# Hybrid decoder block on one core: where the state enters the chunk solve of the gated delta rule, the order of the first loads and masks, and the gate columns' operands

## The reference

```python
proj = xn @ w_in                       # q, k, v, z, and 8 narrow gate columns a, b (4 heads each)
g = -exp(a_log) * softplus(a + dt_bias);  beta = sigmoid(b)
# per chunk, gc = cumsum(g):
T = inverse(I + strict_lower((k * beta) @ k.T * decay))
u = T @ (v * beta)
w = T @ (k * beta * exp(gc))
v_new = u - w @ state
o = (q * exp(gc)) @ state + attn_qk @ v_new
state = state * exp(g_last) + (k * exp(g_last - gc)).T @ v_new
```

## Time and profile before

| | |
|---|---|
| median of three runs | 3064.27 us (3062.66 to 3067.36) |
| the profiled execution: its own time | 3064.6 us |
| its span, first to last instruction | 3062.9 us |
| mean granted clock of PE in it | 0.995 |
| busy: PE, PE's weight loads, DVE, ACT, POOL | 2977.1, 2469.3, 1606.3, 1077.6, 1260.9 us |

### The profile page before, as it was taken

The page is one execution under the profiler, slowest core; times in us unless marked ns, Lnnn a source line. Parts: engine busy times, 40 slices in busy tenths (PEclk is TensorE's granted clock), DMA queues, the critical chain, the costliest instruction groups (busy, mean ns, idle before and its releaser), DMA issues. The chain is left out here.

```text
span 3062.9 us, 42230 instructions
## 1 busy us (share of the span) xinstructions
PE 2977.1 (97%) x14494; PEld 2469.3 (81%) x14494; DVE 1606.3 (52%) x2186; ACT 1077.6 (35%) x1990; POOL 1260.9 (41%) x1126
## 2 busy tenths in 40 slices
PE   6999999999999999999999999999999899999998
PEld 6887788888887888878888878888888788887887
DVE  1454555545357444445565556554635744444445
ACT  4522445424233333332232244443423433332212
POOL 7322444442215444554342244444321454445443
PEclk9999999999999999999999999999999999999999
DMA  6622322241112222252322322214111122225231
GB/s 221 220 89 93 104 69 68 65 163 55 55 69 69 84 84 84 83 192 97 132 92 93 103 93 81 71 62 159 62 43 74 63 82 82 82 82 192 83 110 76
DMA packets 131685, 297.40 MB, mean 97 GB/s; under 512 B 11824, under 2 KB 52848, under 8 KB 131568
## 3 DMA queue, kind: packets, MB, share of 16 engines
q1 hardware_dynamic: 69072, 226.07, 21.3%
q10 hardware_dynamic: 62496, 69.78, 6.6%
HBM read 222.37 MB, written 73.43 MB: 97 GB/s over the span
## 5 line engine op out<-in xcount | busy, mean ns | idle before, releaser
L2385 DVE TENSOR_TENSOR h<-h,PS 128x1024 f32<-128x1024 f32 x272 | 330.9, 1220 | 333.8 <-PE PS L2564 214.8
L2562 PE MATMUL PS<-act_hi,w_hi 128*128 128x512 f32 (+1 forms) x1088 | 428.9, 394 | 10.5 <-POOL w_lo L2027 4.6
L1523 DVE TENSOR_TENSOR copied<-copied,PS 128x512 f32<-128x512 f32 x308 | 207.5, 686 | 400.8 <-PE PS L2564 387.8
L2564 PE MATMUL PS<-act_hi,w_lo 128*128 128x512 f32 (+1 forms) x1088 | 406.7, 374 | 0.0
L2563 PE MATMUL PS<-act_lo,w_hi 128*128 128x512 f32 (+1 forms) x1088 | 405.7, 373 | 0.0
L2013 POOL TENSOR_TENSOR w_lo<-raw,w_hi 128x256 fp32r<-128x256 f32 (+1 forms) x144 | 198.3, 1400 | 433.9 <-ACT w_hi L2104 433.9
L603 POOL TENSOR_TENSOR part_lo<-sum_s,part_hi 128x512 fp32r<-128x512 f32 x176 | 229.9, 1308 | 229.2 <-ACT part_hi L1055 229.2
L2562 PE MATMUL PS<-down,mid 128*128 128x512 f32 x704 | 276.4, 393 | 7.3 <-DVE h L2385 7.3
L2562 PE MATMUL PS<-op_t_hi,part_hi 128*128 128x512 f32 x704 | 275.1, 391 | 0.0
L2564 PE MATMUL PS<-down,mid 128*128 128x512 f32 x704 | 274.8, 390 | 0.0
L2563 PE MATMUL PS<-down,mid 128*128 128x512 f32 x704 | 274.5, 390 | 0.0
(11 more groups left out here) (334 smaller groups left out, 6161.7 us busy)
## 6 DMA issues: line engine op xcount, KB each, us to landing
raw<-in_w_units SPq DMA_DIRECT2D x156, 512.0 KB, 4.0
gu_raw<-in_w_units SPq DMA_DIRECT2D x64, 512.0 KB, 5.0
a_d<-copied SPq DMA_DIRECT2D x88, 256.0 KB, 2.2
mid_raw<-a_d SPq DMA_DIRECT2D x44, 512.0 KB, 4.2
qkvz_d<-stage ACTq DMA_DIRECT2D x64, 256.0 KB, 2.5
raw<-att_d SPq DMA_DIRECT2D x32, 512.0 KB, 3.2
h<-in_x SPq DMA_DIRECT2D x12, 1024.0 KB, 7.9
prep_raw<-in_w_units SPq DMA_DIRECT2D x16, 512.0 KB, 4.4
```

Of the source, the lines that this page charges most:

```text
L1523: dve.tensor_tensor(buf[dst][:, :], buf[a][:, :], bank(k), ALU.add)\
L2385: dve.tensor_tensor(h[:, t, :], h[:, t, :], flat(bank(b + 2 * (t % 2), 2)), ALU.add)\
L2562: nc.tensor.matmul(out_ap, whi, xhi, start=start, stop=False)
L2564: return nc.tensor.matmul(out_ap, wlo, xhi, start=False, stop=stop)
```

## The change

Three edits.

1. **State first.** The step w multiplies the keys `kqn` with `state` into bank 7, four matmuls, and needs nothing of `Xm`. DVE, in the step x6, multiplies the result with nbeg and adds it to `vb`, head by head (four operations). The step v is then `Xm x vb` alone, four matmuls instead of eight. The product `kbg` on DVE and the copy `wt` on ACT are gone.
2. **Start order.** SP loads `mem_in` and `gain` first and the small loads (and `w_ab`) after the first four weight units; ACT takes the statistics of the memory tiles as soon as these two have landed, and splits the first two weight units before the high halves of the memory tiles. POOL makes 14 constants, then goes to the Newton steps and weight halves; masks, `ones_r` and `wab_lo` come after the third Newton step of x. PE starts its transposes after 14 constants.
3. **Gate columns.** High and low part of each row block's eight columns lie side by side in one tile `wab`, so one stationary operand takes both; two matmuls (with `act_hi` and `act_lo`) per row block instead of three. DVE adds the two groups of eight result columns ("sum").

The core of the diff:

```diff
+        def wab_part(hl):
+            return wab[:, 0:KT * 16].rearrange("p (k s c) -> p k s c", s=2, c=8)[:, :, hl, :]
+        def wab_in():
+            return raw[2][:, 0:KT * 8].rearrange("p (k c) -> p k c", c=8)
...
                 if step == "w":
-                    act.wait_ge(S["w_full"], n + 1)
-                    act.wait_ge(S["vn_full"], n)
-                    act.activation(hflat(wt[:, :, :]), bank(7), ACT.Copy).then_inc(S["wt_ready"], 1)
                     if not last:
                         exp_decays(act, n + 1, 1 - par)
...
+            parts = bank(6, 2).rearrange("p b (t c) -> p (b t) c", t=4)
+            step("copy", lambda: dve.tensor_copy(gate_ab[:, :, :], parts[:, :, 2 * NH:4 * NH]))
+            step("sum", lambda: dve.tensor_tensor(gate_ab[:, :, :], gate_ab[:, :, :],
+                                                  parts[:, :, 0:2 * NH], ALU.add))
...
             dve.wait_ge(S["rn_ready"], n + 1)
-            dve.wait_ge(S["gram_full"], n)
+            dve.wait_ge(S["ks_full"], n)
...
+                if step == "x6":
+                    dve.wait_ge(S["ks_full"], n + 1)
+                    for hh in range(NH):
+                        last_rest = dve.scalar_tensor_tensor(
+                            vb[:, hh, :], r4(bank(7))[:, hh, :],
+                            G["nbeg"][:, bass.ds(m, 1), hh:hh + 1].rearrange("p n h -> p (n h)"),
+                            vb[:, hh, :], ALU.mult, ALU.add)
+                    last_rest.then_inc(S["vrest_ready"], 1)
                 if step == "x1":
-                    dve.wait_ge(S["kt_full"], n + 1)
-                    dve.wait_ge(S["w_full"], n)
-                    dve.tensor_tensor(kbg[:, :, :], r4(bank(7)), gate("nbeg", m), ALU.mult)\
-                        .then_inc(S["kbg_ready"], 1)
...
             if step == "w":
-                pe.wait_ge(S["x_ready"], (n + 1) * LEVELS)
-                pe.wait_ge(S["kbg_ready"], n + 1)
+                pe.wait_ge(S["s_ready"], n * 4)
...
                 for hh in range(NH):
-                    t = nc.tensor.matmul(r4(bank(7))[:, hh, :], kbg[:, hh, :], Xm[:, hh, :],
+                    t = nc.tensor.matmul(r4(bank(7))[:, hh, :], kqn[:, hh, 0, :], state[:, hh, :],
                                          start=True, stop=True)
...
             if step == "v":
                 pe.wait_ge(S["ym_ready"], (n + 1) * 12)
-                pe.wait_ge(S["wt_ready"], n + 1)
-                pe.wait_ge(S["s_ready"], n * 4)
+                pe.wait_ge(S["x_ready"], (n + 1) * LEVELS)
+                pe.wait_ge(S["vrest_ready"], n + 1)
                 for hh in range(NH):
-                    nc.tensor.matmul(r4(bank(3))[:, hh, :], Xm[:, hh, :], vb[:, hh, :],
-                                     start=True, stop=False)
-                    t = nc.tensor.matmul(r4(bank(3))[:, hh, :], wt[:, hh, :], state[:, hh, :],
-                                         start=False, stop=True)
+                    t = nc.tensor.matmul(r4(bank(3))[:, hh, :], Xm[:, hh, :], vb[:, hh, :],
+                                         start=True, stop=True)
...
+            sp.dma_start(mem_in[:, :, :], mem.rearrange("(t p) c -> p t c", p=P))\
+                .then_inc(S["gain_in"], 16)
             sp.dma_start(gain[:, :], g_mem[0:1, :].broadcast_to([P, D])).then_inc(S["gain_in"], 16)
...
             for n in range(4 * KT):
+                if n == 4:
+                    load_small()
...
+            pool.wait_ge(made(), FIRST_CONSTS)
+            newton(pool, 0, 0)
+            newton(pool, 1, 1)
+            for n in range(2 * KT):
+                split_lo_prep(n, n % RING)
+            for t in range(3):
+                newton(pool, norm_no(0, 0, t), t % 2)
+            build_masks()
+            pool.wait_ge(S["wab_hi_ready"], 3)
+            pool.tensor_tensor(wab_part(1), wab_in(), wab_part(0).bitcast(f32), ALU.subtract)\
+                .then_inc(S["wab_lo_ready"], 1)
...
+            for t in range(3, TT):
+                newton(pool, norm_no(0, 0, t), t % 2)
...
             act.preload_act_table_set("natural_log_exp_and_others")
-            act.wait_ge(S["const_in"], 8 * 16)
...
+            act.wait_ge(S["gain_in"], 2 * 16)
             for t in range(2):
                 norm_stats(mem_in[:, t, :], junk[:, :], t, t)
-            for t in range(2):
-                norm_hi(t, 0)
...
                 split_hi_prep(n, n % RING)
+                if n == 1:
+                    for t in range(2):
+                        norm_hi(t, 0)
...
+            act.wait_ge(S["const_in"], 7 * 16)
+            act.activation(nega[:, :], nega[:, :], ACT.Exp).then_inc(S["wab_hi_ready"], 1)
...
-            pe.wait_ge(S["const_made"], CONSTS + 1)
+            pe.wait_ge(S["const_made"], FIRST_CONSTS)
...
                     for k in range(KT):
-                        ks = slice(k * 8, k * 8 + P)
+                        ks = slice(k * 16, k * 16 + P)
                         cs = slice(c * CH, (c + 1) * CH)
-                        last = three(PS[:, 4 + c, :], wab_hi[:, ks], wab_lo[:, ks],
-                                     act_hi[:, k, cs], act_lo[:, k, cs], k == 0, k == KT - 1)
+                        nc.tensor.matmul(PS[:, 4 + c, :], wab[:, ks], act_hi[:, k, cs],
+                                         start=k == 0, stop=False)
+                        last = nc.tensor.matmul(PS[:, 4 + c, :], wab[:, ks], act_lo[:, k, cs],
+                                                start=False, stop=k == KT - 1)
```

More of the change, by code:

```diff
@@ L52 @@
 CONSTS = 36
+FIRST_CONSTS = 14
 GD = {n: i + 1 for i, n in enumerate(
-    "copy a neg min bmin w1 wm eq mx rc l1 l2 l3 sp g b1 b2 gc gl fd nb nn".split())}
+    "copy sum a neg min bmin w1 wm eq mx rc l1 l2 l3 sp g b1 b2 gc gl fd nb nn".split())}
 GATE_DVE = len(GD)
@@ L132, in block_kernel @@
         gain = sb("gain", [P, D])
-        wab_hi = sb("wab_hi", [P, KT * 8 + P], f32r)
-        wab_lo = sb("wab_lo", [P, KT * 8 + P], f32r)
+        wab = sb("wab", [P, KT * 16 + P], f32r)
         cw = sb("cw", [P, NH, 3, 4])
@@ L208, in block_kernel @@
         am = sb("am", [P, 2, NH, P // 2], at=z)
-        kbg = sb("kbg", [P, NH, P], at=z)
+        z[0] += NH * P * 4
         kdec = sb("kdec", [P, NH, P], at=z)
@@ L497, in gains @@
         def gains(half, which):
-            return 16 * (2 + NORM_ORDER.index((half, which)))
+            return 16 * (3 + NORM_ORDER.index((half, which)))
         def transposed(half, which):
@@ L1361, in chunk_dve @@
                 if step == "x2":
+                    dve.wait_ge(S["kt_full"], n + 1)
                     dve.wait_ge(S["kv_full"], n)
@@ L1984, in _ @@
                 n += 1
[L1987 to L1995, removed]
-                n += 1
[L1997 to L2000, removed]
-                triangle(v, 2 * b - 1, [[2 * b, m], [0, b]], -1)
-                n += 1
@@ L2003, in _, with build_masks @@
-            pool.memset(Ym[:, :, :], 0.0).then_inc(made(), 1)
-            n += 1
-            assert n == CONSTS
+            def build_masks():
+                n = FIRST_CONSTS
+                for l in range(LEVELS):
+                    b = 1 << l
+                    m = P // (2 * b)
+                    if l == 0:
+                        v = first_mask[:, :].rearrange("p (m e c) -> p m e c", e=2, c=b)[:, :, 0, :]
+                    else:
+                        v = even_mask[:, l - 1, :].rearrange("p (m c) -> p m c", c=b)
+                    pool.wait_ge(made(), n)
+                    pool.memset(v, 1.0).then_inc(made(), 1)
+                    n += 1
+                    pool.wait_ge(made(), n)
+                    triangle(v, -b, [[-2 * b, m], [0, b]], 1)
+                    n += 1
+                    pool.wait_ge(made(), n)
+                    triangle(v, 2 * b - 1, [[2 * b, m], [0, b]], -1)
+                    n += 1
+                pool.memset(Ym[:, :, :], 0.0).then_inc(made(), 1)
+                n += 1
+                assert n == CONSTS
+                pool.tensor_copy(ones_r[:, :], ones[:, :]).then_inc(made(), 1)
@@ L2159, in _ @@
             act.preload_act_table_set("natural_log_exp_and_others")
-            act.wait_ge(S["const_in"], 8 * 16)
-            act.activation(nega[:, :], nega[:, :], ACT.Exp).then_inc(S["wab_hi_ready"], 1)
-            act.wait_ge(S["wab_hi_ready"], 1)
-            act.activation(nega[:, :], nega[:, :], ACT.Copy, scale=-1.0)\
-                .then_inc(S["wab_hi_ready"], 1)
-            act.activation(wab_hi[:, :], raw[2][:, 0:KT * 8 + P], ACT.Copy)\
-                .then_inc(S["wab_hi_ready"], 1)
+            act.wait_ge(S["gain_in"], 2 * 16)
             for t in range(2):
                 norm_stats(mem_in[:, t, :], junk[:, :], t, t)
-            for t in range(2):
-                norm_hi(t, 0)
             def split_hi_prep(n, slot):
@@ L2183, in _ @@
                 split_hi_prep(n, n % RING)
+                if n == 1:
+                    for t in range(2):
+                        norm_hi(t, 0)
```

(8 more changed lines are left out.)

52 lines of the change are left out of this document (21 added, 31 removed).

## The result

The changed kernel takes 3042.11 us (median of 4 runs, 3040.86 to 3043.22) beside 3064.31 us for the kernel before on the same chip: a ratio of 0.9929, with a 95% interval of 0.9915 to 0.9942, so 22.2 us or 0.7% less. Measured once more on another occasion it was 3042.21 beside 3063.13 us. The forecast was 3040.5, the range 3032 to 3050.

The account below looks back on a forecast made before the run. PE, busy 2977.1 of 3062.9 us, was taken as the bound, with only 86 us of waiting to gain. Start -5.1, gate columns -7.4 and chunks -11.2 sum to -23.7 us, from 3064.27 to a predicted 3040.5; range 3032 to 3050.

Parts of the forecast that it names:

- Gate columns: Gate stretch on PE: 16 matmuls fewer per half, 32 in all, at 0.232 us each; -7.4 us.
- Start: Start of the kernel: PE's first 256-column matmul at 18.7 instead of 24.08 us; -5.1 us in all, bounds -3.8 and -6.2.
- Chain after: ... 7.9 + 10.7: Start: gain landed at 7.9 us, plus the old 10.7 us from statistics to second tile's low half, gives 18.6.
- The +0.3 that I allowed: Start: moved POOL masks may hold DVE's `h` normalisation for one POOL operation; +0.3 us.
- v: Step v in the chunks: four of eight matmuls removed, 0.89 us per chunk, 14.2 us for 16 chunks.
- Waiting at v: PE waits at v for DVE's four additions, 0.1 us in each of 14 chunks; +1.4 us.
- State in the odd chunks: Odd chunks: `state` ends just in time for PE's value transposes, 0.1 us in each of six; +0.6 us.
- State in the even chunks: Even chunks: existing waits for `state`, 2.8 us in all, may shrink; counted as a bound only.
- Last chunks: Last chunk of each half: no filler covers the wait at v, +0.5 us twice; +1.0 us.
- shared transfers: Rival, start: gain's load shares transfer engines with four weight loads, start term becomes about +1, time 3047 us; chance 0.08.
- DVE late in the odd chunks: Rival, chunks: DVE's queue becomes late, each of 14 chunks loses another 0.6 to 0.9 us, 3049 to 3053; chance 0.13.
- the four additions never wait for GpSimd: Rival, chunks: each of the four additions waits out one POOL instruction, kernel gets slower, 3078 us; chance 0.03.

Follow-up runs that it names:

- split-held: The changed kernel with GpSimd's first weight split held until VectorE has normalised both memory tiles; 3041.85 us beside 3042.21 for the changed kernel.
- masks-first: The changed kernel with GpSimd's 22 mask operations and `ones_r` back at the head of its queue; 3044.19 us.
- one-slice: The changed kernel with one of the two filler slices between w and v moved ahead of w, in 12 chunks; 3053.39 us.
- chunks-only: The kernel before with only the state-first edit of the chunks (w, four additions, v); 3054.40 us beside 3061.96 for the kernel before.
- after-again: The changed kernel itself, measured once more as reference; 3042.21 us beside 3063.13 for the kernel before.
- tap-and-fill: The changed kernel with last tap and halo copy ahead of the wait for w in odd chunks, and the common filler list in last chunks; 3038.18 us.
- all-three: The changed kernel with tap and halo copy ahead of the wait, common filler list in last chunks, and GpSimd's first split held; 3035.80 us.

## Why the prediction was right, point by point

The time was right to 1.6 us, and each part saves time in the way that was forecast. The closeness is partly luck. By PE's rows the three parts give -3.2 - 7.5 - 9.5 = -20.2 us, 3.5 less than the forecast -23.7. The start and v were taken 1.9 and 1.3 us too large, the last chunks lacked a term of 3.1, and the odd chunks 0.5; `state` in the even chunks gave 2.5 that were counted at nothing. The rest up to the -21.4 of the two profiles is made of things that the sum did not contain: less time at the low clock (-1.8), which no edit explains, the idle at 1734 us (+1.3) and what is not placed (-0.7).

- **Gate columns**: forecast -7.4, found -7.5. 32 matmuls at 0.231 us.
- **Start**: forecast -5.1, found -3.2. The loads (7.71 against 7.9) and the masks' cover were right. What failed is the step "Chain after: ... 7.9 + 10.7": it took the chain of before at its old length, though the change moves GpSimd's splits from behind this chain into it. The second `xn` tile takes 2.06 us more beside the first split; split-held removes exactly this, and in masks-first it moves along with the split. How many of PE's first matmuls run slowly was not in the sum either: 22 for 14, 0.75 us. The +0.3 that I allowed was for the masks beside `h`, the wrong pair: that `h` took 1.28 us as alone (69.84).
- **v**: forecast -14.2, found -12.9. Eight matmuls in one run took 1.78 us, four take 0.97 up to the next step, so 0.81 us are saved per chunk and not half of 1.78.
- **Waiting at v**: forecast 1.4 in 14 chunks, found 1.1 in the twelve chunks of the common filler list, while the two first chunks got 0.3 shorter. one-slice confirms the margin of zero that the term rests on.
- **State in the odd chunks**: forecast +0.6, found +1.1. From gram to the value transposes it is 2.37 us behind chunk 1 (399.09 to 401.46) and was 2.17 (410.71 to 412.88); this is PE held for `state`, which ends at 401.41.
- **State in the even chunks**: forecast 0 with a bound of -2.8, found -2.5. The cause is where `ost_t` falls between GpSimd's operations, as its 0.63 for 1.05 us shows; in one-slice it is 1.06 again and the 2.8 are back.
- **Last chunks**: forecast +1.0, found +1.0 at v. Not priced at all: +3.1 behind them, from the tap and the halo copy that now run beside GpSimd. The prediction named both in the queue behind the additions, but followed that queue in chunk 1 only. The last chunk has another list of fillers and another operation on GpSimd.

Together -12.9 + 1.1 - 0.3 + 1.1 - 2.5 + 1.0 + 3.1 = -9.4 against the forecast -11.2 (PE's rows give -9.5).

None of the rivals happened in full. The gain's load landed 6.4 us after its issue though four weight loads were queued behind it, so the start was not held by shared transfers. DVE late in the odd chunks costs 0.2 us a chunk and not 0.6 to 0.9. And the four additions never wait for GpSimd: in every one of the 16 chunks the four take 1.12 or 1.13 us together.

That last point and the stretches have one explanation that the rows support. The additions have one operand in PSUM and keep their distance of 0.28 us beside GpSimd; `xn` reads `mem_in` and `gain`, both in SBUF, and took 3.34 us. The times fit a turn-taking: GpSimd's first split needs some 2.3 us from 12.77, and 1.28 us more make 16.35, where VectorE is done at 16.20; and the two splits together take 5.64 us instead of the 4.67 of the earlier trace rows, longer by most of VectorE's 1.28. The Trainium skill's "SBUF — State Buffer", section "Who interferes with whom", describes this: the second to come to the shared ports waits until the first is through, and a copy or a `tensor_scalar` in SBUF can need them as well. The halo copy of 128x2 elements, 2.31 us instead of 0.17 beside `mix_even_lo`, agrees, and so does `ost_t` above, a `tensor_scalar`. The prediction had cited this rule, without that exception for operations with one input, and applied it to the chunks only; the first place where it changed the time was the start.

## What to carry to other kernels

When a change moves an engine's work earlier, list what the other engines do in that stretch and which of them share its ports, before taking the old chain at its old length; this cost 2 us at the start and 3 us behind the last chunks. Follow a new wait's queue in each variant of the loop body, the peeled last one above all, since its filler and its neighbours differ. And after the new order is in place, look whether independent operations (here a tap and a copy) can stand in front of the wait: with the filler list and the held split that gave another 5.6 to 6.4 us (3035.80 against 3042.21, on two chips).

## What was not expected of the hardware

TensorE's granted clock falls to 0.50, 1.2 GHz, for 3.4 to 10.2 us at a time and comes back by itself. In the kernel before it does so after an idle of 1.58 us:

```profile
286.89 0.66 PE L2562 MATMUL PS<-act_hi,w_hi 128*128 128x512 f32 x1 [1.58 <-issue]
```

```profile
287.00:288.00 1.00, 1.00 (x3) 0.50 0.19 76
288.00:289.00 1.00, 1.00 (x3) 0.50 0.49 186
289.00:290.00 1.00, 1.00 (x4) 0.50 0.00 0
```

The changed kernel has an idle of 1.44 us at the same matmul and no such stretch; in its second profile it has one. While PE has work, a profiled run has three to seven such stretches, most of them at or behind idles of 1.6 to 3.4 us near 75, 280, 920, 1340, 2370 and 2800 us. Half of their length, an estimate of what they cost a busy PE, is 8.5 to 13.7 us a run (11.9 in the kernel before, 10.2 in the changed one), in no order that follows the edits. The slow matmuls at PE's start come on top: 10 (chunks-only) to 26 (after-again, tap-and-fill, all-three) of them run 0.21 us apart instead of 0.12, a scatter of up to 1.5 us. Only split-held's profile shows a granted clock for them, and there it is 0.50, 1.2 GHz:

```profile
19.00:21.00 2.00, 2.00 (x12) 0.50 0.63 186
```

That the others are at 1.2 GHz too is read from the same distance.

The scatter of both kinds has the size of the effects looked for here, so the waits and distances in the traces carry the argument and not differences of 2 us between medians.
